# Smaller, landed transfers and fewer TensorE instructions in the scan stage of a hybrid RWKV-7 / RG-LRU / mixture-of-experts layer

## The reference, cut to what matters

```
def rwkv7_scan(inputs, s0):
    def step(s, inp):
        r_t, w_t, k_t, v_t, kk_t, a_t = inp
        sa = jnp.einsum('bhvk,bhk->bhv', s, -kk_t)
        s = (s * w_t[:, :, None, :] + sa[..., None] * (kk_t * a_t)[:, :, None, :]
             + v_t[..., None] * k_t[:, :, None, :])
        return s, jnp.einsum('bhvk,bhk->bhv', s, r_t)
...
def block_diag_linear(z, w, bias):
    y = jnp.einsum('bthi,hij->bthj', z.reshape(b, t, LRU_BLOCKS, LRU_BLOCK_DIM), w)
    return y.reshape(b, t, LRU_WIDTH) + bias
...
    rg = jax.nn.sigmoid(block_diag_linear(xc, lp['wa'][d], lp['ba'][d]))
    ig = jax.nn.sigmoid(block_diag_linear(xc, lp['wx'][d], lp['bx'][d]))
```

## Time and profile before

| | |
|---|---|
| runs | median 4354.61 us of 3 (4348.41 to 4357.37) |
| profiled execution | 4352.81 us, span 4351.0 us |
| TensorE busy over the span | 3732.7 us (86%) |
| stage `scan` in the span | about 1117 us to 2436 us |
| granted TensorE clock, mean | 0.928 |

### The profile page before, as it was taken

How to read it: one execution, slowest core, us unless ns; L and a number is a source line. 1 busy time by engine, 2 the same in 40 slices (tenths; PEclk the granted TensorE clock), 3 DMA queues, 4 the chain that set the end, 5 groups by cost and what they waited for, 6 DMA issues and landing times. The chain is left out here.

```text
span 4351.0 us, 118962 instructions
## 1 busy us (share of the span) xinstructions
PE 3732.7 (86%) x50925; PEld 3292.5 (76%) x50925; DVE 2396.6 (55%) x4390; ACT 1828.6 (42%) x2997; POOL 1242.1 (29%) x1250
## 2 busy tenths in 40 slices
PE   4799999999688888888888589795499999999992
PEld 2678888888577777777777488673399999999992
DVE  3246766610256666666666655334766666666664
ACT  3246666521144444444445443231144444444444
POOL 2223333311345555555453155000001010101010
PEclk7899999999899999999899799897699999999996
DMA  5235555522432333332331475341267676767675
GB/s 172 69 125 180 181 172 176 172 95 73 116 76 73 91 81 83 86 86 78 86 81 43 145 224 171 115 153 50 93 196 213 207 213 194 214 197 222 196 213 198
DMA packets 566347, 610.27 MB, mean 140 GB/s; under 512 B 65938, under 2 KB 471252, under 8 KB 564820
## 3 DMA queue, kind: packets, MB, share of 16 engines
q1 hardware_dynamic: 515540, 487.01, 36.4%
q0 software_dynamic: 21536, 76.56, 6.1%
q10 hardware_dynamic: 28768, 39.16, 2.8%
HBM read 443.09 MB, written 159.40 MB: 138 GB/s over the span
## 5 line engine op out<-in xcount | busy, mean ns | idle before, releaser
L339 DVE TENSOR_TENSOR moe_w_lo<-moe_w_lo_whole,moe_w_hi 128x2048 fp32r<-128x2048 f32 (+1 forms) x258 | 453.5, 1758 | 263.2 <-ACT moe_w_hi L517 187.8
L460 PE MATMUL moe_h<-moe_xt_hi,moe_w_hi 128*128 128x256 f32 x2048 | 582.1, 284 | 16.3 <-DVE moe_xt_lo L339 15.0
L460 PE MATMUL moe_h<-moe_xt_lo,moe_w_hi 128*128 128x256 f32 x2048 | 580.2, 283 | 0.0
L460 PE MATMUL moe_h<-moe_xt_hi,moe_w_lo 128*128 128x256 f32 x2048 | 580.1, 283 | 0.0
L1792 PE MATMUL inward_pp<-u_u_hi,inward_w_hi 128*128 128x512 f32 (+1 forms) x1360 | 527.6, 388 | 20.8 <-POOL inward_w_lo L1952 20.8
L1792 PE MATMUL inward_pp<-u_u_lo,inward_w_hi 128*128 128x512 f32 (+1 forms) x1360 | 516.1, 379 | 0.0
L1792 PE MATMUL inward_pp<-u_u_hi,inward_w_lo 128*128 128x512 f32 (+1 forms) x1360 | 515.8, 379 | 0.0
L460 PEld LDWEIGHTS moe_h<-moe_xt_hi,moe_w_hi 128*128 128x128 f32 x2048 | 393.2, 192 | 28.7 <-issue 25.0
L460 PEld LDWEIGHTS moe_h<-moe_xt_lo,moe_w_hi 128*128 128x128 f32 x2048 | 393.4, 192 | 3.8
L460 PEld LDWEIGHTS moe_h<-moe_xt_hi,moe_w_lo 128*128 128x128 f32 x2048 | 393.3, 192 | 0.0
L412 POOL DMA_INDIRECT scratch_x<-moe_ys,moe_who x32 | 70.6, 2205 | 911.0 <-DVE moe_ys L568 906.1
(11 more groups left out here) (376 smaller groups left out, 9924.8 us busy)
## 6 DMA issues: line engine op xcount, KB each, us to landing
moe_w_lo_whole<-in_moe_w SPq DMA_DIRECT2D x387, 512.0 KB, 5.1
scratch_ops<-inward_ops SPq DMA_DIRECT2D x72, 514.0 KB, 3.8
scan_over<-scratch_ops SPq DMA_DIRECT2D x72, 512.0 KB, 9.9
inward_w_lo_whole<-in_w_in SPq DMA_DIRECT2D x38, 512.0 KB, 4.5
scan_aq<-scratch_ops SPq DMA_DIRECT2D x36, 516.0 KB, 5.0
scratch_gates<-inward_out SPq DMA_DIRECT2D x64, 256.0 KB, 2.1
all_late<-in_w_mod POOLq DMA_DIRECT2D x32, 512.0 KB, 5.1
rest_modsum<-scratch_gates SPq DMA_DIRECT2D x64, 256.0 KB, 3.9
```

What stands on the lines that cost most here:

```text
L339: return nc.vector.tensor_tensor(x_lo, x, x_hi.bitcast(F32), ALU.subtract)
L460: mm = nc.tensor.matmul(hb[ft % 2][m][:, 0:CAP], w_, x, start=(k == 0 and part == 0), stop=(k == KD - 1 and part == 2))
```

## The change

Six edits, all in `scan`. On SyncE, `ob`, `over` and `aq` are loaded in pieces of 256 KB (`over` and `aq` once for each direction d), ten pieces for `ob` and `over` and four for `aq`, and SyncE waits after each for its landing before it issues the next; `store(it)` now waits for its own writes after each pair `u`, and it stands ahead of `reload_own(it)`. On GpSimd a piece of `w_mod` is loaded as two halves, each asked for when the half before it in the same place is used up; on ScalarE `raw` is loaded in four parts. On TensorE rounds 1 and 2 become `joint`: round 1 does `B` of pair 0 alternating with `K` of pair 1, round 2 `K` of pair 0 with `B` of pair 1. The product of the identity with the state, which added S to the new state in the bank, is gone: ScalarE makes `Sd`, the state times its decay, and VectorE adds it when it takes the new state out. The gate product is two 64x64 blocks in place of one 128x128 product with zeros.

```
+        FIRST_OF, EVICTED = ("BK", "KB"), {"B": ("W0", "Lb"), "K": ("La", "Lk")}
+        second_done = [EVICTED[FIRST_OF[u][1]][1] + "1" for u in U]
+
+        PE = [Steps(n.sem(f"pe_solve{u}"), ["L", "Lt"] + list(FIRST_OF[u]) + ["tB", "V", "tK"] + level_pe) for u in U]
         AC = steps("act_solve", ["L", "tB", "V", "tK"] + [f"F{m}" for m in LEVELS])
-        DV = steps("dve_solve", ["T0"] + [f"{x}{d}" for x in ("W0", "Lb", "La", "Lk") for d in U] + [f"{x}{m}" for m in LEVELS for x in "TW" if m < 5 or x == "W"])
+        DV = [Steps(n.sem(f"dve_solve{u}"), ["T0"] + [f"{x}{d}" for p in FIRST_OF[u] for x in EVICTED[p] for d in U] +
+                    [f"{x}{m}" for m in LEVELS for x in "TW" if m < 5 or x == "W"]) for u in U]
...
-            def load(it, own, rest):
+            def load_own(it, wait):
                 src = env["ops"][:, it]
                 for u in U:
-                    if own:
-                        sp.dma_start(aq[u][:, it % 2, :, :], src[u][:, :, 2 * G:4 * G + 4]).then_inc(s_aq[u][it % 2], 16)
-                    if rest:
-                        sp.dma_start(ob[u][:, :, :], src[u][:, :, 4 * G + 4:OPS]).then_inc(s_ob[u], 16)
-                        sp.dma_start(over[u][0:HD, :, :], src[u][HD:P, :, 0:4 * G]).then_inc(s_over0[u], 16)
-                        sp.dma_start(over[u][HD:P, :, :], src[u][0:HD, :, 0:4 * G]).then_inc(s_over1[u], 16)
+                    for d in range(2):
+                        sp.dma_start(aq[u][:, it % 2, d, :], src[u][:, d, 2 * G:4 * G + 4]).then_inc(s_aq[u][it % 2], 16)
+                        if wait:
+                            sp.wait_ge(s_aq[u][it % 2], 32 * (it // 2) + 16 * d + 16)
+
+            def load(it, wait):
+                src = env["ops"][:, it]
+                for u in U:
+                    sp.dma_start(ob[u][:, :, :], src[u][:, :, 4 * G + 4:OPS]).then_inc(s_ob[u], 16)
+                    if wait:
+                        sp.wait_ge(s_ob[u], 16 * it + 16)
+                for d in range(2):
+                    for u in U:
+                        sp.dma_start(over[u][0:HD, d, :], src[u][HD:P, d, 0:4 * G]).then_inc(s_over0[u], 16)
+                        if wait:
+                            sp.wait_ge(s_over0[u], 32 * it + 16 * d + 16)
+                        sp.dma_start(over[u][HD:P, d, :], src[u][0:HD, d, 0:4 * G]).then_inc(s_over1[u], 16)
+                        if wait:
+                            sp.wait_ge(s_over1[u], 32 * it + 16 * d + 16)
 
             def reload(it):
                 for u in U:
                     PE[u].wait(sp, "tK", it)
-                load(it + 1, False, True)
+                load(it + 1, True)
 
             def reload_own(it):
                 for u in U:
                     PEc[u].wait(sp, "Y3", it)
                     DVc[u].wait(sp, "Sb3", it)
-                load(it + 2, True, False)
+                load_own(it + 2, True)
...
+                    sp.wait_ge(s_y[u], 64 * (it + 2))
 
             n_main = sum(k for _, k in CONST_SIZES)
-            load(0, True, True)
+            load_own(0, False)
+            load(0, False)
             sp.dma_start(masks[:, :], t["consts"][:, n_main:n_main + len(MASKS) * P]).then_inc(s_masks, 16)
-            load(1, True, False)
+            load_own(1, False)
             reload(0)
             for it in range(LAST + 1):
                 if it + 2 <= LAST:
                     reload(it + 1)
+                store(it)
+                if it + 2 <= LAST:
                     reload_own(it)
-                store(it)
-            for u in U:
-                sp.wait_ge(s_y[u], 64 * (LAST + 2))
...
-            def both_of(name, u, lhs, rhs, first, across):
+            def side_by_side(u, k, lhs, rhs, first, across):
+                d, c = k // 4, k % 4
+                for h, other in zip(HALVES, HALVES[::-1]):
+                    moving = rhs[h, d, first:first + 2 * G].rearrange("p (x t) -> p x t", x=2)[:, :, c * HD:(c + 1) * HD]
+                    to = bank[u][2 + d][other if across else h, 2 * c * HD:2 * (c + 1) * HD].rearrange("p (x f) -> p x f", x=2)
+                    mm = nc.tensor.matmul(to, lhs(h, k), moving, start=True, stop=True)
+                return mm
+
+            def joint(r, a):
+                it, b, half = a
+                uB, uK = (0, 1) if r == 1 else (1, 0)
+                for u in U:
+                    if r == 1:
+                        AC[u].wait(pe, "L", it)
+                        DV[u].wait(pe, "T0", it)
+                    else:
+                        DV[u].wait(pe, EVICTED[FIRST_OF[u][0]][1] + "1", it)
+                pe.wait_ge(s_over0[uK], 32 * it + 32)
+                pe.wait_ge(s_over1[uK], 32 * it + 32)
                 for k in range(8):
-                    d, c = k // 4, k % 4
-                    for h, other in zip(HALVES, HALVES[::-1]):
-                        moving = rhs[h, d, first:first + 2 * G].rearrange("p (x t) -> p x t", x=2)[:, :, c * HD:(c + 1) * HD]
-                        to = bank[u][2 + d][other if across else h, 2 * c * HD:2 * (c + 1) * HD].rearrange("p (x f) -> p x f", x=2)
-                        mm = nc.tensor.matmul(to, lhs(h, k), moving, start=True, stop=True)
-                PE[u].did(name, mm)
+                    mmB = side_by_side(uB, k, of_ops(ob[uB], None, 0), aq[uB][:, b], 0, False)
+                    mmK = side_by_side(uK, k, of_ops(over[uK], None, G), over[uK], 2 * G, True)
+                PE[uB].did("B", mmB)
+                PE[uK].did("K", mmK)
...
-                    pe.wait_ge(s_aq[u][b], half * 16 + 16)
+                    pe.wait_ge(s_aq[u][b], half * 32 + 32)
...
-                elif r == 1:
-                    AC[u].wait(pe, "L", it)
-                    DV[u].wait(pe, "T0", it)
-                    both_of("B", u, oB, aq[u][:, b], 0, False)
-                elif r == 2:
-                    pe.wait_ge(s_over0[u], 16 * it + 16)
-                    pe.wait_ge(s_over1[u], 16 * it + 16)
-                    DV[u].wait(pe, "Lb1", it)
-                    both_of("K", u, xK, over[u], 2 * G, True)
                 elif r == 3:
-                    DV[u].wait(pe, "Lk1", it)
+                    DV[u].wait(pe, second_done[u], it)
...
-                    mm = nc.tensor.matmul(bank[u][0][:, G:2 * G], wbd[:, u, :], xc[:, k % 2, :], start=True, stop=True)
+                    for h in HALVES:
+                        mm = nc.tensor.matmul(bank[u][0][h, G:2 * G], wbd[h, u, :], xc[h, k % 2, :], start=True, stop=True)
...
-                        nc.tensor.matmul(region(0, 1, d, h), stack[h, :], S[u][h, c % 2, d, :], start=False, stop=False)
...
+                    for d, at in ((0, c), (1, 3 - c)):
+                        ACc[u].did(f"D{'ab'[d]}{c}", act.activation(Sd[u][:, d, :], S[u][:, c % 2, d, :], ACT.Copy, scale=aq[u][:, it % 2, d, 2 * G + at:2 * G + at + 1]))
...
-                    act.dma_start(raw[:, CTX:], src[:, LAT0:LAT0 + SEQ]).then_inc(s_lat, 16)
+                    n_ = SEQ // 4
+                    act.dma_start(raw[:, CTX + part * n_:CTX + (part + 1) * n_], src[:, LAT0 + part * n_:LAT0 + (part + 1) * n_]).then_inc(s_lat, 16)
...
-                    PE[u].wait(dve, "BK"[r - 1], it)
-                    for name, x, part, mask in ((("W0", W[u], 0, "lev0"), ("Lb", Lb[u][b], 1, "nincl")) if r == 1 else
+                    product = FIRST_OF[u][r - 1]
+                    PE[u].wait(dve, product, it)
+                    for name, x, part, mask in ((("W0", W[u], 0, "lev0"), ("Lb", Lb[u][b], 1, "nincl")) if product == "B" else
                                                 (("La", La[u][b], 0, "strict"), ("Lk", Lk[u][b], 1, "incl"))):
...
+                    ACc[u].wait(dve, f"Db{c}", it)
                     for d, at in ((0, c), (1, 3 - c)):
-                        D.did(f"S{'ab'[d]}{c}", dve.tensor_scalar(S[u][:, (c + 1) % 2, d, :], bank[u][0][:, (2 + d) * HD:(3 + d) * HD],
-                                                                 aq[u][:, b, d, 2 * G + at:2 * G + at + 1], None, ALU.mult))
+                        D.did(f"S{'ab'[d]}{c}", dve.scalar_tensor_tensor(out=S[u][:, (c + 1) % 2, d, :], in0=bank[u][0][:, (2 + d) * HD:(3 + d) * HD],
+                                                                        scalar=aq[u][:, b, d, 2 * G + at:2 * G + at + 1], in1=Sd[u][:, d, :], op0=ALU.mult, op1=ALU.add))
...
-            def load(part_):
+            def load(part_, x):
                 if part_ < 4 * KD:
-                    at, half = part_ // 2, part_ % 2
-                    pool.dma_start(wm, w_mod[:, NJ * half:NJ * (half + 1), 2 * D + at * G:2 * D + (at + 1) * G]).then_inc(s_wm, 16)
+                    at, k = part_ // 2, NJ * (part_ % 2) + NJ // 2 * x
+                    pool.dma_start(wm[:, NJ // 2 * x:NJ // 2 * (x + 1), :], w_mod[:, k:k + NJ // 2, 2 * D + at * G:2 * D + (at + 1) * G]).then_inc(s_wm[x], 16)
```

41 lines of the change are left out of this document (25 added, 16 removed).

## The result

The changed kernel took 4451.57 us (median of 4 runs, 4445.89 to 4455.13) against 4355.99 us before (4 runs, 4348.41 to 4364.31): a ratio of 1.0218, with a 95% interval of 1.0196 to 1.024. It is slower by 2.2%, outside the range predicted and on the other side of the kernel before. The profiled execution took 4445.89 us.

A forecast was written before the change was run, and what follows sets the result against it. TensorE sets the pace before; SyncE's serial circle was to become the bound at 71.5 us a body. From 4352.8 us, 6 off the sixteen bodies and 17 outside give 4329.8, with the median's offset 4332; range 4255 to 4412.

The forecast's parts named there:

- SyncE's circle: SyncE's serial loads and writes, from one tK to the next, become the new bound: 71.5 us a body.
- A landed 256 KB load: Each of SyncE's landed pieces takes 3.0 us (bounds 2.7 and 3.4): ten take 30 us, four 12 us.
- rival 1: SyncE's circle is longer: at 3.4 us a piece, 77.1 us a body and 4422 us; chance 0.20.
- the sum outside the circle: Iteration 0, the solve of iteration 17 and the last states keep TensorE's gains: 17 us less.
- The writes: SyncE's landed writes of y: 4.1 us, twice, so 8.2 us a body in SyncE's circle.
- `L` to `tK`: TensorE's stretch from product L to the end of tK, slow start included: 21.3 us a body.
- The issue gaps: TensorE's waits for late instruction refills, 10.5 us a body, shrink with small transfers, to below 4 us.
- Rival 4: TensorE's gaps aren't the refills' lateness and stay: body 76 us, time 4412 us; chance 0.09.
- identity product: Dropping its 64 TensorE records a body saves 1.9 us.
- Gates: Eight gate products a body as 64x64 blocks save TensorE 2.3 us in all.
- Joint rounds: B and K of both pairs run 3.5 us shorter on TensorE, 2.6 return as a wait; net gain 0.5 us.
- The state update's "I take 0": VectorE's changed instruction and ScalarE's sixteen small ones a body fit in those engines' slack: 0 us.

The follow-up runs named there:

- e2: Changed kernel with SyncE's queue of before (pieces, waits and order undone), against the kernel before: 4303.3 us, ratio 0.9875.
- e1: Kernel before with only the changed SyncE queue (landed 256 KB pieces, y's stores ahead of aq): 4486.6 us, ratio 1.0287 to the kernel before.
- e8: e2 with the identity product of the state put back: 4340.3 us, ratio 0.9971 to the kernel before.
- e9: e6 with the joint rounds undone, each pair's B and K by itself: 4181.7 us, ratio 0.9596 to the kernel before.
- e7: e2 with the joint rounds undone, each pair's B and K by itself: 4291.9 us, ratio 0.9856 to the kernel before.
- e13: Changed kernel with aq landed in 516 KB and over in 512 KB pieces, waits and order kept: 4395.6 us, ratio 1.0091 to the kernel before.
- e4: Changed kernel with all landing waits of SyncE's queue taken out, same pieces and order: 4299.2 us, ratio 0.9866 to the kernel before.
- e6: Changed kernel with aq's loads ahead of y's stores and two pieces in flight: 4205.3 us, ratio 0.9651 to the kernel before.
- e12: Kernel before with only SyncE's queue changed: 256 KB pieces, two in flight, aq ahead of y's stores: 4239.5 us, ratio 0.9737 to the kernel before.

## Why the prediction was wrong

- **What bounds the changed kernel: right.** TensorE has time left, SyncE's circle sets the body, and TensorE waits for `aq` in one place (15.5 us a body, where some 11 were named). `L` of pair 1 began 0.04 us after the last `aq` landed, on average.
- **The step that failed: "I take 3.0 with the wake of SyncE in it (bounds 2.7 and 3.4)", in *A landed 256 KB load*.** The eight pieces of `over` took 3.7, above the upper bound, and `ob`'s two 3.2: the ten took 36.8 us instead of 30. That alone is 6.8 of the 6.9 us by which the body was longer. `aq`'s four took 2.7, the lower bound: 11.0 instead of 12. I had seen that `over` writes only 64 partitions, and raised the value by that to 3.0; the nearest row, `ob` at 3.3 in this stage, should have been the middle and not the upper end. With 3.4, rival 1 had the body at 77.1 and the time at 4422. Pieces above 3.4 us apart were one of the prediction's own signs of being wrong. In the price were missing the 64 partitions at their full 0.7 us and the instruction packets that most pieces of `over` move beside (the sorting above). Of the 120 us between forecast and result the sixteen bodies are 104, 6.5 each, and the sum outside the circle 13.
- **The writes: 9.7 against 8.2.** They landed after 2.6 us, where the earlier trace rows has 2.2. `aq` and the writes cancel.
- **`L` to `tK`: right**, 20.8 against 21.3, the slow start at half clock in it.
- **The sum outside the circle: wrong.** 17 us were to be gained there. `L` of iteration 1 came 4.3 us earlier (1190.9 to 1186.6); from `L` of iteration 17 to the end of the scan's products nothing came: 94.9 us before, 95.9 after. The prediction had that nothing waits for SyncE there; but `L` of pair 1 of iteration 17 still waited 3.4 us for `aq`, and the solve began at half clock, as every other. With the old queue (e2) this stretch was 89.2 us.
- **The issue gaps: right in cause, too much in size.** Fewer bytes in flight take them away (e1: 5.7 us a body, 7.5 were expected), to 4.7 and 5.4 us, not below 4. Rival 4, that they stay, is out: 5.7 us a body hung on SyncE's transfers alone, and the gaps follow late instruction packets. The rule named there (the Trainium skill, "Runtime: NRT & Kernel Launch", section Instruction fetch mechanics), that the cost of such refills is mostly hidden, holds by count and not by cost: in the kernel before, 41 of some 245 packets were followed by a gap of over 1 us, but those gaps were 8.2 us of a body of 71.9.
- **Terms of TensorE: identity product right** (e8). **Gates right in one reading**: in e9 a gate product began at 1702.24 and the next product at 1702.68, 0.44 us, and the start of the one before lay 0.11 us ahead instead of 0.26, in all 8 x (0.63 + 0.26 - 0.44 - 0.11) = 2.7 a body against 2.3. The time shows less: e7, with the identity product gone, the gates in blocks and the loads cut, gained 63 us by its ratio, and e8 puts 42 of them on the identity product. Some 20 us, 1.2 a body, are left for gates and loads together. The reading:

```profile
1702.13 0.33 PE L2380 MATMUL scan_b<-scan_S,scan_aq 64*64 64x64 f32 x4
1702.24 0.65 PE L2385 MATMUL scan_b<-all_late,scan_wbd 64*64 64x256 f32 x4
1702.68 0.33 PE L2379 MATMUL scan_b<-scan_V,scan_La 64*64 64x64 f32 x4
```

- **Joint rounds wrong in sign**: 0.5 us a body was expected as a gain (its own terms, 3.5 less 2.6, make 0.9), it was a loss of 0.8 to 1.4 (e7, e9). The wait before round 2, 2.4 us, was as said (2.6); the saving was 2.2 or less instead of 3.5, and the waits for `Z` and the clock were not in the sum.
- **The state update's "I take 0"** holds within e8. TensorE did come to wait 1.2 us a body for VectorE's `Z`, but that hangs on the joint rounds too: 0.7 us are left with the identity product back (e8), under 0.2 with the joint rounds undone (e7, e9).
- **The rule weighed.** A landed 258 KB of `aq` took 2.66 us in the changed kernel. The estimate of 2.6 us from the Trainium skill, "DMA: Bandwidth & Descriptors", section Anatomy of one DMA, agrees with it and is a third too low for `over`; for 512 KB it gives an estimated 3.2 us where e13 had 5.0. The page fits its figures for the software path of GpSimd, while the profile lists SyncE's loads under a hardware queue (`q1 hardware_dynamic`), so they need not carry over. In e13 256 KB more cost 1.3 us, about 200 GB/s. Its section Bandwidth spoke against the cut, and e13, with twice the size landed, was 56 us faster than the changed kernel; but e4 and e6 show no harm from small pieces when the next is already under way.

The forecast's margin was thin: 71.5 us against 71.9, decided at 0.1 us a piece, while one piece's value was known to 0.7. It gave this side 0.24. The chance of rival 1 should have been at least that of the sum.

## What to carry to other kernels

A transfer that is waited for before the next is issued costs its whole latency, so count the circle of the queue and not its bytes; two in flight took most of the latency out (20 us for ten pieces instead of 37) and kept TensorE's instruction fetch almost as free (issue gaps of 5.9 us a body in e12, 4.7 in e1). Order a serial queue by who waits: loads that the next product needs go ahead of writes that nobody does (124 us here for two lines). And when a forecast hangs on a latency that no row shows in that form, give the upper end of the nearest rows as much weight as the middle.
